# Feed-forward up product of a two-block transformer kernel: weights as the stationary operand, high and low tokens side by side as 512 moving columns

## The reference

```
def swiglu_ffn(h, w_gu, w_down):
    gate, up = jnp.split(h @ w_gu, 2, axis=-1)       # D_FF = 2816
    return (jax.nn.silu(gate) * up) @ w_down

for i in range(2):
    x = x + 0.5 * swiglu_ffn(rms_norm(x, norm_g[i, 0]), ffn_w_gu[i, 0], ffn_w_down[i, 0])
    h = rms_norm(x, norm_g[i, 1])
    x = x + (gla_mixer if i == 0 else diff_mixer)(h, ...)
    x = x + 0.5 * swiglu_ffn(rms_norm(x, norm_g[i, 2]), ffn_w_gu[i, 1], ffn_w_down[i, 1])
```

## Time and profile before

| | before |
|---|---|
| median of 3 executions | 1894.45 us (1893.42 to 1896.24) |
| the profiled execution | 1896.12 us |
| its span, first to last instruction | 1894.3 us |
| PE busy | 1857.4 us, 98% |
| DVE busy | 1203.7 us, 64% |
| ACT busy | 998.8 us, 53% |
| HBM read | 312.18 MB |

### The profile page before, as it was taken

One profiled execution on the slowest core, in us unless ns is written; L12 is line 12 of the kernel. 1 busy time (PEld: TensorE's weight loads), 2 busy tenths in 40 slices (PEclk: granted clock), 3 DMA queues, 4 the chain that ended last, 5 costly groups with the idle time before them and its releaser, 6 DMA issues.

```text
span 1894.3 us, 27430 instructions
## 1 busy us (share of the span) xinstructions
PE 1857.4 (98%) x9936; PEld 1567.7 (83%) x9936; DVE 1203.7 (64%) x1707; ACT 998.8 (53%) x1538; POOL 124.0 (7%) x119
## 2 busy tenths in 40 slices
PE   9999999999999999899999999999999999999998
PEld 7888778888888888778888988888888889989886
DVE  5555696555555557765556865787765657766864
ACT  5444686544444455754445454667465643435553
POOL 1000000000000002200000000104320112100000
PEclk9999999999999999999999999999999999999999
DMA  7556444565576555246555565544135654346553
GB/s 231 185 178 187 132 145 153 183 187 185 188 248 206 185 183 167 89 139 194 186 185 172 176 198 175 172 144 123 57 110 171 184 170 135 119 132 191 178 179 122
DMA packets 215657, 314.73 MB, mean 166 GB/s; under 512 B 16658, under 2 KB 115192, under 8 KB 215552
## 3 DMA queue, kind: packets, MB, share of 16 engines
q1 hardware_dynamic: 212704, 306.76, 51.4%
q0 software_dynamic: 2784, 6.52, 1.1%
q10 hardware_dynamic: 64, 0.02, 0.0%
HBM read 312.18 MB, written 3.16 MB: 166 GB/s over the span
## 4 chain that ended last, share of the span: by engine, by line
PE 91%; DVE 5%; ACT 3%; issue 1%; DMA 0%; SPq 0%; DVEq 0%; ACTq 0%
PE acc L850 51%; PE acc L855 25%; PE tp L810 4%; PE acc L873 2%; PE acc L878 1%; DVE arena L2515 1%; DVE w_lo L2339 1%; ACT arena L1620 1%; PE mx L1407 1%; PE tp L1407 1%; PE mx L1499 1%; PE mx L1500 1%; DVE x L2411 1%; PE tp L1520 0%; DVE norm_lo L2358 0%
## 5 line engine op out<-in xcount | busy, mean ns | idle before, releaser
L2339 DVE TENSOR_TENSOR w_lo<-w_raw,w_hi 128x1024 fp32r<-128x1024 f32 (+1 forms) x565 | 682.8, 1220 | 407.1 <-ACT w_hi L1594 404.7
L1594 ACT ACTIVATE w_hi<-w_raw 128x1024 fp32r<-128x1024 f32 (+1 forms) x589 | 612.3, 1048 | 519.1 <-PE acc L855 446.9
L850 PE MATMUL acc<-w_hi,norm_hi 128*128 128x512 f32 x1344 | 427.3, 399 | 2.1 <-DVE norm_lo L2358 1.5
L850 PE MATMUL acc<-w_hi,norm_lo 128*128 128x512 f32 x1344 | 415.8, 391 | 0.0
L855 PE MATMUL acc<-w_lo,norm_hi 128*128 128x512 f32 x1344 | 359.1, 390 | 1.1 <-DVE w_lo L2339 1.1
L850 PEld LDWEIGHTS acc<-w_hi,norm_lo 128*128 128x128 f32 x1344 | 253.0, 189 | 53.6
L855 PEld LDWEIGHTS acc<-w_lo,norm_hi 128*128 128x128 f32 x1344 | 252.2, 189 | 54.5 <-DVE w_lo L2339 2.0
L850 PEld LDWEIGHTS acc<-w_hi,norm_hi 128*128 128x128 f32 x1344 | 245.5, 189 | 51.7 <-issue 2.8
L850 PE MATMUL acc<-w_hi,inner_hi 128*128 128x512 f32 (+1 forms) x880 | 271.7, 390 | 4.5 <-DVE inner_lo L2358 4.5
L850 PE MATMUL acc<-w_hi,inner_lo 128*128 128x512 f32 (+1 forms) x880 | 266.9, 384 | 0.0
L855 PE MATMUL acc<-w_lo,inner_hi 128*128 128x512 f32 (+1 forms) x880 | 230.4, 384 | 0.0
(11 more groups left out here) (353 smaller groups left out, 1528.8 us busy)
## 6 DMA issues: line engine op xcount, KB each, us to landing
w_raw<-in_ffn_w_gu SPq DMA_DIRECT2D x352, 256.0 KB, 3.0
w_raw<-in_ffn_w_down SPq DMA_DIRECT2D x88, 512.0 KB, 4.4
w_raw<-in_pool_w_in SPq DMA_DIRECT2D x64, 512.0 KB, 4.5
w_raw<-in_gdn_w_in SPq DMA_DIRECT2D x48, 512.0 KB, 3.9
w_raw<-in_pool_w_out SPq DMA_DIRECT2D x32, 512.0 KB, 4.2
w_raw<-in_mla_w_in SPq DMA_DIRECT2D x26, 512.0 KB, 3.8
w_raw<-in_gla_w_in SPq DMA_DIRECT2D x24, 512.0 KB, 3.6
w_raw<-in_diff_w_in SPq DMA_DIRECT2D x24, 512.0 KB, 4.4
```

The costliest lines, as they stand in the source:

```text
L850: pe.matmul(acc_of(g, i, part, tok, 0, w), t[:, tile * SEQ + tok * P:tile * SEQ + (tok + 1) * P], b_hi, start=t is hi and k + kk == 0, sto ...
L1594: act.activation(slot(w_hi, g, i, p, 0, n), slot(w_raw, g, i, p, 0, n), ACT.Copy).then_inc(S["rounded"], 1)
L2339: dve.tensor_tensor(slot(w_lo, g, i, p, 0, n), slot(w_raw, g, i, p, 0, n), slot(w_hi, g, i, p, 0, n).bitcast(F32), ALU.subtract).then_inc( ...
```

## The change

The up product alone is computed turned: the weight piece of 128x128 is stationary, and the tokens move, so that the outcome has features on partitions and needs no turn. `norm_hi` and `norm_lo` become the halves of one tensor, `norm_both`; with `w_hi` stationary one matmul moves 256 high and 256 low tokens (two runs, 2048 elements apart) into the two halves of a bank. With `w_lo` stationary 256 high tokens move. A block takes four banks: even blocks the whole of `acc`, odd blocks `mx` and `tp`. The first half of the down product goes to `mx`. ACT copies the low halves of the four banks out, DVE adds the high halves, and 1/rms is now a row along the tokens, which must be made first: DVE writes `wide`, PE sums it with the identity (`rows_under`, L1000), ACT copies it (L1772).

```diff
+            def ffn_pair(i, kind):
+                tile = acc[:, kind * 2 * BANK:(kind + 1) * 2 * BANK] if like(i) % 2 == 0 else (mx, tp)[kind][:, :]
+                return tile.rearrange("p (c a t) -> p a c t", c=2, a=2)
...
# PE
-                product(up, 0, norm_t, need=need)
-                        product(up, At(2 * r + n + 1, n + 1), norm_t)
-                        turn_act(At(2 * r + n, n))
-                finish(down, inner_t, need=last_of(u0), between=lambda p: turn_act(UP - 1) if p == 0 else None)
+                def block(i, need=None, between=None):
+                    tile = lambda c: ffn_pair(i, c // 2)[:, :, c % 2, :]
+                    for p, (_, k, nk, _) in enumerate(up.chunks):
+                        pe.wait_ge(S["rounded"], up.chunk(i, p) + 1)
+                        for kk in range(nk):
+                            if need is not None and kk % 2 == 0:
+                                need(k + kk)
+                            both = norm_both[:, :].rearrange("p (a n) -> p a n", a=2)[:, :, (k + kk) * SEQ:(k + kk + 1) * SEQ]
+                            for c in range(BANK // P):
+                                pe.matmul(tile(c), slot(w_hi, up, i, p, kk * BANK + c * P, P), both, start=k + kk == 0, ...)
+                        wait_split(pe, up, i, p)
+                        for kk in range(nk):
+                            for c in range(BANK // P):
+                                last = pe.matmul(tile(c)[:, 0, :], slot(w_lo, up, i, p, kk * BANK + c * P, P),
+                                                 norm_hi[:, (k + kk) * SEQ:(k + kk + 1) * SEQ], start=False, ...)
...
+                def rows_under(p):
+                    if p == 2:
+                        see["ffn_wide_ready"].take(pe)
+                        for tok in range(TT):
+                            last = pe.matmul(bank(mx, 0, tok * P, P), ffn_t["wide"][...], ident[:, :], start=True, stop=True)
+                        see["ffn_row_sum"].up(last)
+                        if st == bias_stage:
...
+                    if p == 2 and first_product[st].before is None:
+                        turn_rows()
+                for n in (1, 2):
+                    if up.block0 >= n:
+                        wait_evacuated(pe, *plan.block_at[up.block0 - n])
+                block(0, need_x, rows_under)
+                see["ffn_row_ready"].take(pe)
...
# ACT
-                    for tok in range(TT):
-                        last = act.activation(silu[...], acc_of(up, i, 0, tok, 0, SEQ), ACT.Silu, scale=rstd[:, tok:tok + 1])
-                        hi_part(inner_t, 2 * (2 * r + n))
+                    act.activation(ffn_t["gate"]..., ffn_pair(i, 0)[:, 1], ACT.Copy)
+                    see["ffn_half_ready"].up(act.activation(ffn_act(i)..., ffn_pair(i, 1)[:, 1], ACT.Copy))
+                    see["ffn_gate_ready"].take(act)
+                    see["ffn_silu_ready"].up(act.activation(ffn_t["gate"], ffn_t["gate"], ACT.Silu))
+                    see["ffn_act_ready"].take(act)
+                    see["ffn_hi_ready"].up(act.activation(inner_hi[...], ffn_act(i), ACT.Copy))
...
# DVE
-                    for tok in range(TT):
-                        last = dve.scalar_tensor_tensor(out=act_t[:, at_tok], in0=acc_of(...), scalar=rstd[...], in1=silu[...], ...)
-                        lo_part(inner_t, 2 * (2 * r + n))
+                    step.up(dve.tensor_tensor(gate, ffn_pair(i, 0)[:, 0], gate, ALU.add))
+                    last = dve.tensor_tensor(act_i, ffn_pair(i, 1)[:, 0], act_i, ALU.add)
+                    last.then_inc(S["dve_evac"], 1)
+                    see["ffn_gate_ready"].up(dve.tensor_tensor(gate, gate, row, ALU.mult))
+                    step.up(dve.tensor_tensor(act_i, act_i, row, ALU.mult))
+                    see["ffn_act_ready"].up(dve.tensor_tensor(ffn_act(i), ffn_t["gate"], ffn_act(i), ALU.mult))
+                    see["ffn_lo_ready"].up(dve.tensor_tensor(inner_lo[...], ffn_act(i), inner_hi[...], ALU.subtract))
```

More of the change, by code:

```diff
@@ L387, in acc_of @@
         def acc_of(g, i, part, tok, off=0, n=BANK):
+            if g.in_mx and number(i) == 0:
+                return bank(mx, tok, off, n)
             b = (g.odd(i, part) * 2 + tok) * BANK + off
@@ L1702, in ffn, with copy_half @@
                 norm(st)
[L1703 to L1705 removed]
+                def copy_half(i):
                     wait_block(act, up, i)
[L1707 to L1712 removed]
@@ L2470, in ffn @@
+                see["rstd_ready"].wait(dve)
+                for tok in range(TT):
+                    last = dve.tensor_scalar(ffn_t["wide"][:, tok * P:(tok + 1) * P], one[:, 0:1].to_broadcast([P, P]),
+                                             rstd[:, tok:tok + 1], None, ALU.mult)
+                see["ffn_wide_ready"].up(last)
+                feed.to(up.chunk(0, 2) + SLOTS)
                 if first_product[st].before is None:
                     see["rows_turned"].take(dve)
-                    see["gains_ready"].up(dve.tensor_copy(gains[:, norm_rows:GAINS], mx[:, norm_rows:GAINS]))
+                    see["gains_ready"].up(dve.tensor_copy(gains[:, norm_rows:GAINS], bank(mx, 1, norm_rows, GAINS - norm_rows)))
```

144 lines of the change are left out of this document (91 added, 53 removed).

## The result

| | before | changed |
|---|---|---|
| median (7 executions each) | 1896.05 us | 1902.93 us |
| lowest to highest | 1893.42 to 1896.69 | 1901.60 to 1903.20 |
| the profiled execution | 1896.12 us | 1902.49 us |
| its span | 1894.3 us | 1900.7 us |
| PE, DVE, ACT busy | 98%, 64%, 53% | 98%, 69%, 55% |

A forecast was written before the change was run, and what follows sets the result against it. It took the kernel to be bound by what PE issues, busy 98%. 12.0 us gained less 9.7 lost at first blocks made 2.3 less: 1893.8 for the profiled execution, 1892.1 us as median, 0.12% faster; range 1883 to 1899.

The forecast's parts named there:

- The term of a block: Up product: 32 matmuls at 0.2267 and 32 at 0.120 us make a block 11.09 us, 0.254 less than before.
- two runs cost more: Rival, up product: each of 1408 wide matmuls takes 0.0133 us longer, 18.8 us in all, giving 1910.9 us; 8%.
- the gain of the turns: Feed-forward stages: dropping the blocks' turns and the new block time save 3.01 us a stage, 12.0 over four.
- the clock falls in ffn0: Rival: PE's 3.3 us without work in ffn0 lowers the granted clock, losing 3.1 us of work, giving 1895.2 us; 22%.
- the sum: Whole kernel: 12.0 us gained, 9.7 lost at the first blocks, 2.3 less, giving 1892.1 us; 56% as it stands.
- the loss at the first block: Block 1 starts late by 3.24 us in ffn0, 2.61 in ffn1, 1.28 in ffn2 and 2.61 in ffn3.
- sum and turn: ffn0, after the wait for `wide`: the row's sum takes 0.43 us and the gains' turn about 0.3.
- the three waits for the residual: PE idle before the first matmul of ffn1, ffn2 and ffn3 by 2.0, 1.5 and 2.0 us, released by DVE's residual.
- the wait of 3.4 and its releaser: Sign: PE idle 3.4 us before the row's sum in ffn0, released by DVE's `wide`, and none in the other three.
- the evacuation: Blocks' copies and adds on ACT and DVE cost nothing, 3.1 us to spare; rival that they bound: 22 us, 1914; 4%.

The follow-up runs named there:

- one_run: Changed kernel, but each 512-column matmul of the up product streams one contiguous run of high parts, low parts left out: 1902.95 us, ratio 1.0036 to the kernel before.
- all_wide: Changed kernel, but the 256-column matmuls of the up product stream high and low parts too, so all 64 of a block have 512 columns: 2046.06 us.
- filled: Changed kernel with matmuls nobody reads in PE's stops: thirteen in ffn0, six at the start of ffn1, ffn2 and ffn3: 1897.55 us, ratio 1.0006 to the kernel before.
- sum_late: Changed kernel, but in ffn0 the row's sum and its wait for `wide` stand behind block 0's fourth chunk: 1901.10 us, ratio 1.0028 to the kernel before.
- before_wait_2: Kernel before with an added PE wait for the norm's reciprocal ahead of ffn0 block 0's fourth chunk, second profile: 1901.06 us.

## Why the prediction was wrong

**The term of a block.** The step "I take 0.2267, since the array takes the same columns and the output of each is one whole bank in order" failed in size: 0.2300 was measured, inside the bounds given (0.2267 to 0.240), and the narrow ones took 0.119. A block is 11.18 in place of 11.09 us, 44 x 0.09 = 4.0 us. The rival "two runs cost more" had its point of decision at 1.6 ns a matmul; the block's extra 0.09 over 32 wide ones is 2.8 ns, beyond it. But its mechanism is not the one: two runs cost nothing (`one_run`, `all_wide`); the two widths in turn do. I had priced each width from a stream of that width alone, and the sum over two streams was taken for the price of their mixture. This term was mis-sized; the gain of the turns in it held.

**The clock.** The step was the weight of the rival "the clock falls in ffn0", 22%, with the argument "the rows show the low level with PE busy, and none after a stop". No row of before could show that, since PE has no such stop in a dense stretch there: it was absence of a case, and I read it as evidence. So the sum had the clock at nothing. The fall came and cost 2.4 us (`filled`) where the rival had 3.1. A second one behind ffn1's stop of 1.86 us costs 1.56 (188.26 against 186.70 in `filled` and in `sum_late`, which has the stop and no fall), and there the prediction had no clock term at all, though it forecast that stop. At the start of ffn3 the same stop of 1.9 us brought no fall in any profile; what sets these two apart is open.

**The rest of the sum** held. By stage, the profile of changed less that of before against the forecast:

| | forecast | measured | pitch | clock | left |
|---|---|---|---|---|---|
| ffn0 | +0.23 | +3.01 | 1.0 | 2.4 | -0.6 |
| ffn1 | -0.40 | +2.23 | 1.0 | 1.56 | +0.1 |
| ffn2 | -1.73 | -0.62 | 1.0 | | +0.1 |
| ffn3 | -0.40 | +0.62 | 1.0 | | 0.0 |

(Forecast: the loss at the first block less 3.01; pitch: 11 x 0.09; clock: from `filled`; left: measured less the other three.) In ffn0, `wide` was ready at 22.2 instead of 23.0, as everything lay 0.76 us earlier in this execution, and the other way sum and turn take 1.01 us (`filled`) and not 0.73, 0.3 more; that explains 0.5 of the -0.6. The gain of the turns, the three waits for the residual (1.86, 1.38 and 1.89 against 2.0, 1.5 and 2.0), the wait of 3.4 and its releaser, and the evacuation that never shows up are as worked out. Of the 10.8 us between 1892.1 and 1902.93 the four stages make 7.5 (+5.2 where -2.3 was forecast). Another 1.6 is the kernel before: its three executions had a median of 1894.45, its seven have 1896.05. The last 1.7 are gla and diff, which add 1.0 between the two profiles and had no term in the sum, and what the profiled executions differ from their medians.

**The range.** Each rival was laid on the sum alone. Two losses came together, one by a mechanism that no rival had: 4.0 us of pitch and 4.0 of clock (2.4 and 1.6), and with both 1892.1 becomes 1900.1, past an upper end of 1899 that held either one. The clock's low level fits the Trainium skill's rule (TensorE: Matmul & The Clock Gate, What's actually happening) that the lower rate is the default and activity lifts it; the falls behind stops in ffn0 agree with it, 2.4 us by `filled` and 1.7 by `before_wait_2`, and the stop at ffn3, as long as ffn1's and with no fall in eight profiles, shows that not every stop does it. The rival would have deserved the larger chance.

## What to carry to other kernels

Where PE is busy 98% of the time, a new wait can cost more than its length: give a fall of the clock behind it a term of its own, at each place where one is added, or arrange buffers so that the engine never stops. Take the price of a mixed stream from a mixed stream. Follow not only what waits on PE, but what stands ahead of the releaser in its own queue (`sum_late`). And compare two profiles of the same kernel before a difference in a stage that the change doesn't touch is explained.
